# 56 tokens' expert value rows gathered and summed on VectorE instead of 48, in three groups with an accumulator each

## The chip, the cores and the metric

The kernel runs on one core of one Trainium2 chip. The metric is the device time of one execution in microseconds (us). The core has five engines that run their own instruction streams and wait for one another through semaphores: TensorE (PE), VectorE (DVE), ScalarE (ACT), GpSimd (POOL) and SyncE (SP, which here only issues transfers). Transfers run on 16 DMA engines, whichever engine issues them.

## The reference

One decoder layer on 256 tokens of width 1024: a mixer (a gated recurrence and causal attention side by side), cross-attention to 256 memory tokens, and a PEER block, with a final RMSNorm. The change is in PEER, where each token picks, in 8 heads, the 16 best of 128 x 128 = 16384 single-neuron experts:

```
q = (t @ w_q).reshape(T, 8, 2, 128)
s = einsum('thpd,hpnd->thpn', q, sub_keys)        # scores against two sets of 128 keys
ids, gates = top-16 of the 16 x 16 sums of the best 16 of each set; softmax   # 128 ids a token
act = gelu(einsum('td,ted->te', t, u[ids]))        # 128 activations a token
y   = einsum('te,ted->td', gates * act, v[ids])    # sum of 128 value rows a token
```

## The kernel before, in words

Up to about 245 us the kernel computes mixer, cross-attention, queries and key scores; in this part weights are split into a high and a low float32r part, so that three products give float32 accuracy. Then come two passes over all 16384 experts, in 128 steps ("keys") of 128 experts each.

**u pass.** For each key j a 512 KB slab of expert rows is loaded (`raw`, four slots, L373), split into a high part on ACT (L762) and a low part on DVE (L1150), and multiplied with all tokens on PE (L1635 to L1668). ACT applies gelu and leaves activations of the first DT tokens in `act_w` and of the last NS tokens in `act_s`. Meanwhile DVE chooses each token's experts, and POOL scatters the gates of WT = 192 of the tokens into the HBM map `wmap`, with a chain of 192 indirect transfers (L478). The gates of OT = 16 more tokens do not go through the map: PE builds them from one-hots, GRP = 4 tokens at a time (`route`, L1660; `onehots_i`, `onehots_j`, `place`, `late_gelu`).

**v pass.** For each key j a slab of value rows is loaded (L406, issued four keys ahead, when the slab's slot is split), split by ACT (L762) and DVE (`split_low`, L1143), and PE adds, in 8 chunks of 128 output columns, value rows times weighted activations: a matmul of 2 x DT columns (L1702, high and low activations at once) and one of DT columns (L1703, the low part of the rows), 208 each time before the change. The weighted activations are made two keys at a time: SP loads a block of the map (`wblk`, L397), DVE multiplies it in (`weigh`, L1272), ACT and DVE split the product (`a_high` L814, `a_low` L1264). DVE's order for step j is: at odd j `weigh`, then `split_low` of key j + 4, at even j `a_low`, then at some steps one `sparse_fma`.

**The NS sparse tokens** (48 before) do not go through PE. Their 128 experts each are laid out over 128 partitions, so that one column c holds 128 (token, expert) choices: NSD = NS columns. For each column POOL gathers 128 value rows from HBM, 512 KB in all, into one of three slots (`vg`, L501), and one activation for each choice out of the dump of `act_s` (`aw_s`, L492); DVE adds weight times row to an accumulator (L1284, a fused multiply-add; the first column of a group L1286). POOL issues two activation gathers ahead of each value gather until all are out, and starts on `vg` of column c when the sum of column c - 3 is done. When DVE takes a column is fixed by the step:

```
def fma_step(c):
    return FMA0 + c * (KEYS - 8 - FMA0) // NSD      # FMA0 = 12, KEYS = 128
```

There are two groups, of 32 and 16 tokens: a token's choices then lie on 4 or on 8 partitions. After the last column two transfers and two additions fold both accumulators into one (L416, L1342), and in key KEYS - 3 a float32 matmul of 48 columns per chunk sums over the partitions with the 0/1 matrix `sel` (L1724). The last two keys are done chunk by chunk with three matmuls of DT columns each (L1713), followed by residual, norm and output.

**What orders the start of the v pass.** POOL waits until all scatters have landed, then loads the first two map blocks (L486); DVE's first two `weigh` wait for them, and PE's first v matmul for what ACT and DVE make of them.

Of the kernel before, what the change touches and what calls it, by code (L numbers as in the profile page):

```python
# [15 lines left out]
U32 = mybir.dt.uint32  # L16
# [6 lines left out]
P = 128  # L23
# [34 lines left out]
DVE_EVAC = set(range(U_OUT, U_CV3)) | set(range(U_CO, U_PQ))  # L58

GRP = 4  # L60
NS, NSA = 48, 32
NSB = NS - NSA
DT = T - NS
HT = 64
OT = P - HT - NS
NGRP = OT // GRP
WT = P + HT
NDA, NDB = NSA * PH * TOPK // P, NSB * PH * TOPK // P
NSD = NDA + NDB
ACTB = 8  # L70
DUMP = 8
XR2_KEY = KEYS - 16
# [17 lines left out]
def build(nc, x, mem, par, wa, wx, w, keys_t, u_t, v, wmap, adump, sgate, sidx, xres, out):  # L90
    ctx = ExitStack()
    with ctx:
# [8 lines left out]
        K = 1024  # L101

        act_s = at("act_s", 0, [KEYS, NS])
        act_w = at("act_w", 24 * K, [KEYS, DT])
        vg = at("vg", 0, [NVG, D])
        acc_s = at("acc_s", 12 * K, [2, D])
        shifted = at("shifted", 20 * K, [D])
        fin = at("fin", 24 * K, [DC, T])
        ysq = at("ysq", 32 * K, [DC, T])
        orow = at("orow", 40 * K, [TT, D])  # L110
# [23 lines left out]
        oh_j = at("oh_j", m + 4 * K, [2, GRP, P])  # L134
        m += 8 * K
        kt3 = at("kt3", m, [3, OT])
        gate_s = at("gate_s", m + 192, [NSD])
        idx_v = at("idx_v", m + 384, [NSD], U32)
        idx_a = at("idx_a", m + 576, [NSD], U32)
        late = at("late", m + 768, [2, OT])  # L140
        aw_s = at("aw_s", m + 896, [NSD])
        w_s = at("w_s", m + 1088, [NSD])
        stage_g = at("stage_g", m + 1280, [PH * TOPK])
        stage_i = at("stage_i", m + 1792, [PH * TOPK], U32)
        sel = at("sel", m + 4352, [NS])
# [170 lines left out]
        def vbank(c):  # L316

            return acc[:, c] if c < 4 else bank[c - 4]

        SPARSE = ((P - NS, NSA, 0, NDA), (P - NSB, NSB, NDA, NDB))  # L320

        def placed(j):

# [6 lines left out]
        def _(sp):  # L330
# [40 lines left out]
            for j in range(4, KEYS):  # L371
                sp.wait_ge(s_ul, j - 3)
                sp.dma_start(raw[:, j // 2 % 2, j % 2], u_t[j // 2][:, j % 2]).then_inc(s_raw[j % 4], 16)  # L373
                if j == 88:
                    sp.wait_ge(s_stg, 1)
                    for far, near in ((sgate, stage_g), (sidx, stage_i)):
                        for t0, nt, c0, nc_ in SPARSE:
                            sp.dma_start(far[P * c0:P * (c0 + nc_), :].rearrange("(r t c) o -> t r (c o)", t=nt, c=nc_),
                                         near[t0:t0 + nt, :].rearrange("t (r c) -> t r c", c=nc_)).then_inc(s_sst, 16)
                if j == 96:  # L380
                    sp.wait_ge(s_sst, 64)
                    for far, near in ((sgate, gate_s), (sidx, idx_v)):
                        for t0, nt, c0, nc_ in SPARSE:
                            sp.dma_start(near[:, c0:c0 + nc_],
                                         far[P * c0:P * (c0 + nc_), :].rearrange("(p c) o -> p (c o)", p=P)).then_inc(s_sbk, 16)
                if j % DUMP == 0 and j >= 3 * DUMP:
                    dump(j - 3 * DUMP, j - 2 * DUMP)
                if j == KEYS - 4:
                    dump(KEYS - 3 * DUMP, KEYS - 2 * DUMP)
# [37 lines left out]
        def _(pool):  # L427
# [53 lines left out]

            for k, (_, _, _, nr) in enumerate(SETS):
                pool.wait_ge(s_sca[k], 16 * nr * PH)
            pool.wait_ge(s_sst, 64)
            for p in range(2):
                nc.gpsimd.dma_start(wblk[:, p], wm[:, WBK * p:WBK * p + WBK]).then_inc(s_wbp[p], 16)  # L486
            pool.wait_ge(s_ad, 16 * KEYS // DUMP)
# [393 lines left out]
        def _(dve):  # L881
# [86 lines left out]
            dve.wait_ge(s_const, 11)  # L968
            link(V.tensor_copy(posu[:, 0, 0:1], tcol[:, 0:1]))
            V.tensor_scalar(posu[:, 1, 0:1], posu[:, 0, 0:1], NSA - 1, None, ALU.bitwise_and)  # L970
            link(V.tensor_scalar(posu[:, 1, 1:2], posu[:, 0, 0:1], NSB - 1, None, ALU.bitwise_and))
            V.tensor_copy(tcol[:, 2:3], posu[:, 1, 0:1])
            link(V.tensor_copy(tcol[:, 4:5], posu[:, 1, 1:2]))
            V.tensor_scalar(tcol[:, 5:6], tcol[:, 4:5], float(NSA), None, ALU.add)
            link(V.memset(sel[:], 0.0))
            V.tensor_scalar(sel[0:64, 0:NSA], iota[0:64, 0:NSA], tcol[0:64, 2:3], None, ALU.is_equal)
            V.tensor_scalar(sel[64:P, NSA:NS], iota[64:P, 0:NSB], tcol[64:P, 4:5], None, ALU.is_equal)

            dve.wait_ge(s_spc, 1)
            e, z, z2, q, sp8 = c4(1), c4(2), c4(3), c4(4), c4(5)  # L980
# [293 lines left out]
            def sparse_fma(c):  # L1274
                if c % ACTB == 0:
                    cs = slice(c, min(c + ACTB, NSD))
                    dve.wait_ge(s_ag[c // ACTB], 16 * (cs.stop - cs.start))
                    V.tensor_tensor(w_s[:, cs], gate_s[:, cs], aw_s[:, cs], ALU.mult).then_inc(s_ws, 1)
                    dve.wait_ge(s_ws, c // ACTB + 1)
                dve.wait_ge(s_vg[c % NVG], 16 * (c // NVG + 1))  # L1280
                w, to = w_s[:, c:c + 1], acc_s[:, c // NDA]
                if c % NDA:
                    dve.wait_ge(s_fma, c)
                    V.scalar_tensor_tensor(to, vg[:, c % NVG], w, to, ALU.mult, ALU.add).then_inc(s_fma, 1)  # L1284
                else:
                    V.tensor_scalar(to, vg[:, c % NVG], w, None, ALU.mult).then_inc(s_fma, 1)  # L1286
# [8 lines left out]
            for j in range(KEYS):  # L1295
                if j >= WIDE0:
                    wide_sum(j)
                if HALVES <= j < KEYS - 4:
                    split_low_halves(j % 4, s_ul, (s_uh, j + 5))
                elif j < KEYS - 4:  # L1300
                    split_low(j % 4, s_ul, (s_uh, j + 5))
                elif j < KEYS - 1:
                    split_low(j % 4, s_vl, (s_vh, j + 5 - KEYS), second=True)
                if batches < len(BATCHES) and j == batch_key(batches) + 4:
                    gates(batches)
                    batches += 1
                if parts < 4 * TT * PH and j == part_key(parts):
                    route_part(parts // 4, parts % 4)
                    parts += 1
                if j in range(ROUTE0, ROUTE0 + 2 * NGRP, 2):  # L1310
                    place((j - ROUTE0) // 2)
                if placed(j):
                    late_gelu(j)
                if j == ROUTE0 - 2:
                    dve.wait_ge(s_kte, 1)
                if j == ROUTE0 + 2 * NGRP:
                    dve.wait_ge(s_sbk, 64)
                    for (_, _, c0, nc_), col in zip(SPARSE, (2, 5)):
                        cs = slice(c0, c0 + nc_)
                        last = V.tensor_scalar(idx_a[:, cs], idx_v[:, cs], float(NS), tcol[:, col:col + 1], ALU.mult, ALU.add)  # L1320
                    last.then_inc(s_ix, 1)
                if j + 2 in range(ROUTE0, ROUTE0 + 2 * NGRP, 2):
                    onehots_i((j + 2 - ROUTE0) // 2)
                if j == KEYS - 4:
                    for p in range(2):
                        weigh(p)
                if j == KEYS - 3:
                    for p in range(2):
                        a_low(p)
# [54 lines left out]
        def _(pe):  # L1384
# [336 lines left out]
                return last  # L1721

            def sparse_sum(c):
                pe.matmul(vbank(c)[:, DT:T], acc_s[:, 0, P * c:P * c + P], sel[:], start=False, stop=False, skip_group_check=True)  # L1724

            for j in range(8):
                pe.wait_ge(s_vl, j + 1)
# [76 lines left out]
```

## Time and profile before

| | us |
|---|---|
| median of 3 runs (lowest, highest) | 969.2 (968.04, 970.23) |
| the profiled execution's own time | 968.83 |
| its span, first to last instruction | 967.0 |
| PE busy | 954.4 |
| DVE busy | 806.9 |
| ACT busy | 542.6 |
| POOL busy | 486.4 |

The time of an execution is the span plus 1.83 us around it. Busy times are unions over the whole span. A matmul's duration overlaps the next one's, so what a matmul costs is read from start to start. The granted clock of PE is a share of full speed.

### The profile page before, as it was taken

How to read it: one execution, taken by the hardware profiler on the slowest of the kernel's cores; microseconds unless marked ns; L12 is line 12 of the kernel's file. 1: busy time of each engine (PE TensorE's matmuls, PEld its weight loads, DVE VectorE, ACT ScalarE, POOL GpSimd, SP SyncE). 2: the span in 40 equal slices, each digit the busy share in tenths (PEclk: the TensorE clock that was granted, in tenths of full speed). 3: DMA queues.
4: the chain of work that ended last, by engine and by line, in shares of the span. 5: the costliest groups of instructions: out<-in, count | busy, mean ns of one | idle time of the engine just before them, and what ended most of it. 6: DMA issues, size and time to landing. Idle time of an engine off the chain costs nothing.

```text
span 967.0 us, 18013 instructions
## 1 busy us (share of the span) xinstructions
PE 954.4 (99%) x6807; PEld 915.2 (95%) x6807; DVE 806.9 (83%) x1571; ACT 542.6 (56%) x953; POOL 486.4 (50%) x315
## 2 busy tenths in 40 slices
PE   8999999999999999999999999999999999999997
PEld 8897799999999999999998888889999999999997
DVE  5988866446999999999988787777899899999897
ACT  7775546555555546464465565545555455555456
POOL 1001001001488888888788888827478872242210
PEclk9999999999999999999999999999999999999999
DMA  9699865434547787878878878878999999999992
GB/s 317 218 316 323 269 226 200 147 123 139 175 82 203 180 208 179 213 169 205 202 189 208 194 174 194 201 202 307 329 362 345 338 347 374 361 372 354 366 339 95
DMA packets 134265, 235.61 MB, mean 244 GB/s; under 512 B 38624, under 2 KB 87520, under 8 KB 133824
## 3 DMA queue, kind: packets, MB, share of 16 engines
q1 hardware_dynamic: 97552, 208.66, 64.4%
q0 software_dynamic: 36224, 25.70, 14.1%
q8 instruction: 27, 0.44, 0.2%
q10 hardware_dynamic: 432, 0.57, 0.2%
q14 instruction: 30, 0.25, 0.1%
HBM read 216.38 MB, written 17.97 MB: 242 GB/s over the span
## 4 chain that ended last, share of the span: by engine, by line
PE 51%; POOL 33%; issue 8%; DVE 5%; ACT 2%; DMA 1%; ACTq 0%; POOLq 0%; DVEq 0%
POOL wmap L478 33%; PE acc L1702 11%; PE bank L1702 11%; PE acc L1438 11%; PE bank L1703 5%; PE acc L1703 5%; PE acc L1420 3%; DVE wsp L893 1%; PE acc L1421 1%; PE acc L1424 1%; ACT wsp L511 1%; PE bank L1544 1%; PE bank L1391 1%; DMA wmap<-gate,widx 1%; PE bank L1566 1%
## 5 line engine op out<-in xcount | busy, mean ns | idle before, releaser
L478 POOL DMA_INDIRECT wmap<-gate,widx x192 | 322.3, 1679 | 90.8 <-issue 60.0
L762 ACT ACTIVATE hl<-raw 128x1024 fp32r<-128x1024 f32 x192 | 202.3, 1058 | 80.3 <-PE bank L1668 41.7
L1143 DVE TENSOR_TENSOR hl<-raw,hl 128x1024 fp32r<-128x1024 f32 x99 | 120.9, 1221 | 24.2 <-ACT hl L762 24.1
L1635 PE MATMUL bank<-xt,hl 128*128 128x256 f32 x480 | 136.0, 283 | 0.0
L1636 PE MATMUL bank<-xt,hl 128*128 128x256 f32 x480 | 135.9, 283 | 0.0
L1637 PE MATMUL bank<-xt,hl 128*128 128x256 f32 x480 | 135.9, 283 | 0.0
L501 POOL DMA_INDIRECT vg<-v,idx_v x48 | 74.3, 1549 | 119.0 <-DVE acc_s L1284 99.7
L1150 DVE TENSOR_TENSOR hl<-raw,hl 128x512 fp32r<-128x512 f32 x186 | 119.3, 687 | 17.0 <-ACT hl L762 15.8
L1702 PE MATMUL bank<-whl,hl 128*128 128x416 f32 x380 | 121.1, 369 | 0.7 <-DVE acc L1292 0.7
L1702 PE MATMUL acc<-whl,hl 128*128 128x416 f32 x380 | 121.7, 371 | 0.0
L1667 PE MATMUL bank<-xt,hl 128*128 128x512 f32 x288 | 102.4, 399 | 0.0
L893 DVE TENSOR_TENSOR wsp<-wraw,wsp 128x2048 fp32r<-128x2048 f32 x34 | 77.8, 2289 | 24.6 <-ACT wsp L511 24.3
L1703 PE MATMUL bank<-whl,hl 128*128 128x208 f32 x380 | 98.1, 258 | 0.0
L1703 PE MATMUL acc<-whl,hl 128*128 128x208 f32 x380 | 97.9, 258 | 0.0
L511 ACT ACTIVATE wsp<-wraw 128x2048 fp32r<-128x2048 f32 x35 | 67.0, 1914 | 54.0 <-PE acc L1421 24.6
L1636 PEld LDWEIGHTS bank<-xt,hl 128*128 128x128 f32 x480 | 92.1, 192 | 0.0
L1637 PEld LDWEIGHTS bank<-xt,hl 128*128 128x128 f32 x480 | 92.1, 192 | 0.0
L1635 PEld LDWEIGHTS bank<-xt,hl 128*128 128x128 f32 x480 | 92.0, 192 | 0.0
L1438 PE MATMUL acc<-xt,wsp 128*128 128x256 f32 x672 | 84.0, 285 | 0.1
L772 ACT ACTIVATE act_w<-bank 128x208 f32<-128x208 f32 x80 | 27.6, 344 | 99.1 <-PE bank L1637 98.7
L492 POOL DMA_INDIRECT aw_s<-adump,idx_a x48 | 69.6, 1450 | 26.6 <-issue 14.3
L1438 PEld LDWEIGHTS acc<-xt,wsp 128*128 128x128 f32 x672 | 81.6, 192 | 0.7 <-issue 0.4
(306 smaller groups left out, 2379.6 us busy)
## 6 DMA issues: line engine op xcount, KB each, us to landing
raw<-u_t SPq DMA_DIRECT2D x128, 512.0 KB, 4.5
raw<-v SPq DMA_DIRECT2D x128, 512.0 KB, 5.9
wmap<-zeros SPq DMA_DIRECT2D x6, 2048.0 KB, 11.7
wblk<-wmap SPq DMA_DIRECT2D x62, 192.0 KB, 6.1
wraw<-w_in SPq DMA_DIRECT2D x9, 1024.0 KB, 9.4
wraw<-w_pq SPq DMA_DIRECT2D x8, 1024.0 KB, 5.3
wraw<-w_ck SPq DMA_DIRECT2D x4, 1024.0 KB, 8.4
wraw<-w_cv SPq DMA_DIRECT2D x4, 1024.0 KB, 7.0
```

The costliest lines, as they stand in the source:

```text
L478: nc.gpsimd.indirect_dma_start(out=wmap, out_offset=bass.IndirectOffsetOnAxis(ap=set_ranks(widx, k)[:, h, r:r + 1], axis=0), in_=set_ranks ...
L762: nc.scalar.activation(eslot(k, 0, second), raw[:, k // 2, k % 2], ACT.Copy).then_inc(ready, 1)
L893: V.tensor_tensor(wsp[:, u % 2, 1], wraw[:, u % WRAW], wsp[:, u % 2, 0].bitcast(F32), ALU.subtract).then_inc(s_wl, 1)
L1143: V.tensor_tensor(eslot(k, 1, second), raw[:, k // 2, k % 2], eslot(k, 0, second).bitcast(F32), ALU.subtract).then_inc(ready, 1)
L1150: last = V.tensor_tensor(eslot(k, 1, False)[:, q], raw[:, k // 2, k % 2, q], eslot(k, 0, False)[:, q].bitcast(F32), ALU.subtract)
L1438: last = pe.matmul(dst, a, b, start=(c == c0 and n == 0), stop=(c == c1 - 1 and n == 2))
L1635: pe.matmul(dst, uh[:, c], xt[:, c, 0], start=(c == 0), stop=False)
L1636: pe.matmul(dst, uh[:, c], xt[:, c, 1], start=False, stop=False)
L1637: last = pe.matmul(dst, ul[:, c], xt[:, c, 0], start=False, stop=(c == DC - 1))
L1667: pe.matmul(dst, uh[:, c], flat(xt[:, c]), start=(c == 0), stop=False, skip_group_check=True)
L1702: pe.matmul(both, vh[:, q], whole, start=first, stop=False, skip_group_check=True)
L1703: last = pe.matmul(both[:, 0], vl[:, q], whole[:, 0], start=False, stop=False, skip_group_check=True)
```

## The change

Eight more tokens move from PE to the sparse path: NS goes from 48 to 56, so DT from 208 to 200, and a third group of 8 tokens (each on 16 partitions) gets its own accumulator, staging transfers and columns of `sel`. The tokens placed by one-hots, OT = 128 - 64 - NS, go from 16 to 8, so NGRP from 4 to 2. The map's width WT stays. `sparse_sum` becomes two matmuls, of 48 and of 8 columns, since the third accumulator is not folded into the first. Some tiles move in SBUF. The index step that stood at ROUTE0 + 2 * NGRP = 103 keeps its place as ROUTE0 + 8. `fma_step` is unchanged but divides by the new NSD = 56.

```diff
--- before.py
+++ after.py
@@ -58,15 +58,15 @@
 DVE_EVAC = set(range(U_OUT, U_CV3)) | set(range(U_CO, U_PQ))
 
 GRP = 4
-NS, NSA = 48, 32
-NSB = NS - NSA
+NS, NSA, NSB, NSC = 56, 32, 16, 8
 DT = T - NS
 HT = 64
 OT = P - HT - NS
 NGRP = OT // GRP
 WT = P + HT
-NDA, NDB = NSA * PH * TOPK // P, NSB * PH * TOPK // P
-NSD = NDA + NDB
+NDA, NDB, NDC = (n * PH * TOPK // P for n in (NSA, NSB, NSC))
+NSD = NDA + NDB + NDC
+FIRSTS = (0, NDA, NDA + NDB)
 ACTB = 8
 DUMP = 8
 XR2_KEY = KEYS - 16
@@ -101,10 +101,10 @@
         K = 1024
 
         act_s = at("act_s", 0, [KEYS, NS])
-        act_w = at("act_w", 24 * K, [KEYS, DT])
+        act_w = at("act_w", 28 * K, [KEYS, DT])
         vg = at("vg", 0, [NVG, D])
-        acc_s = at("acc_s", 12 * K, [2, D])
-        shifted = at("shifted", 20 * K, [D])
+        acc_s = at("acc_s", 12 * K, [3, D])
+        shifted = at("shifted", 24 * K, [D])
         fin = at("fin", 24 * K, [DC, T])
         ysq = at("ysq", 32 * K, [DC, T])
         orow = at("orow", 40 * K, [TT, D])
@@ -134,12 +134,12 @@
         oh_j = at("oh_j", m + 4 * K, [2, GRP, P])
         m += 8 * K
         kt3 = at("kt3", m, [3, OT])
-        gate_s = at("gate_s", m + 192, [NSD])
-        idx_v = at("idx_v", m + 384, [NSD], U32)
-        idx_a = at("idx_a", m + 576, [NSD], U32)
+        gate_s = at("gate_s", m + 96, [NSD])
+        idx_v = at("idx_v", m + 320, [NSD], U32)
+        idx_a = at("idx_a", m + 544, [NSD], U32)
         late = at("late", m + 768, [2, OT])
-        aw_s = at("aw_s", m + 896, [NSD])
-        w_s = at("w_s", m + 1088, [NSD])
+        aw_s = at("aw_s", m + 832, [NSD])
+        w_s = at("w_s", m + 1056, [NSD])
         stage_g = at("stage_g", m + 1280, [PH * TOPK])
         stage_i = at("stage_i", m + 1792, [PH * TOPK], U32)
         sel = at("sel", m + 4352, [NS])
@@ -317,7 +317,7 @@
 
             return acc[:, c] if c < 4 else bank[c - 4]
 
-        SPARSE = ((P - NS, NSA, 0, NDA), (P - NSB, NSB, NDA, NDB))
+        SPARSE = ((P - NS, NSA, 0, NDA), (P - NSB - NSC, NSB, NDA, NDB), (P - NSC, NSC, NDA + NDB, NDC))
 
         def placed(j):
 
@@ -378,7 +378,7 @@
                             sp.dma_start(far[P * c0:P * (c0 + nc_), :].rearrange("(r t c) o -> t r (c o)", t=nt, c=nc_),
                                          near[t0:t0 + nt, :].rearrange("t (r c) -> t r c", c=nc_)).then_inc(s_sst, 16)
                 if j == 96:
-                    sp.wait_ge(s_sst, 64)
+                    sp.wait_ge(s_sst, 32 * len(SPARSE))
                     for far, near in ((sgate, gate_s), (sidx, idx_v)):
                         for t0, nt, c0, nc_ in SPARSE:
                             sp.dma_start(near[:, c0:c0 + nc_],
@@ -481,7 +481,7 @@
 
             for k, (_, _, _, nr) in enumerate(SETS):
                 pool.wait_ge(s_sca[k], 16 * nr * PH)
-            pool.wait_ge(s_sst, 64)
+            pool.wait_ge(s_sst, 32 * len(SPARSE))
             for p in range(2):
                 nc.gpsimd.dma_start(wblk[:, p], wm[:, WBK * p:WBK * p + WBK]).then_inc(s_wbp[p], 16)
             pool.wait_ge(s_ad, 16 * KEYS // DUMP)
@@ -968,13 +968,17 @@
             dve.wait_ge(s_const, 11)
             link(V.tensor_copy(posu[:, 0, 0:1], tcol[:, 0:1]))
             V.tensor_scalar(posu[:, 1, 0:1], posu[:, 0, 0:1], NSA - 1, None, ALU.bitwise_and)
-            link(V.tensor_scalar(posu[:, 1, 1:2], posu[:, 0, 0:1], NSB - 1, None, ALU.bitwise_and))
+            V.tensor_scalar(posu[:, 1, 1:2], posu[:, 0, 0:1], NSB - 1, None, ALU.bitwise_and)
+            link(V.tensor_scalar(posu[:, 1, 2:3], posu[:, 0, 0:1], NSC - 1, None, ALU.bitwise_and))
             V.tensor_copy(tcol[:, 2:3], posu[:, 1, 0:1])
-            link(V.tensor_copy(tcol[:, 4:5], posu[:, 1, 1:2]))
+            V.tensor_copy(tcol[:, 4:5], posu[:, 1, 1:2])
+            link(V.tensor_copy(tcol[:, 6:7], posu[:, 1, 2:3]))
             V.tensor_scalar(tcol[:, 5:6], tcol[:, 4:5], float(NSA), None, ALU.add)
+            V.tensor_scalar(tcol[:, 7:8], tcol[:, 6:7], float(NSA + NSB), None, ALU.add)
             link(V.memset(sel[:], 0.0))
             V.tensor_scalar(sel[0:64, 0:NSA], iota[0:64, 0:NSA], tcol[0:64, 2:3], None, ALU.is_equal)
-            V.tensor_scalar(sel[64:P, NSA:NS], iota[64:P, 0:NSB], tcol[64:P, 4:5], None, ALU.is_equal)
+            V.tensor_scalar(sel[64:P, NSA:NSA + NSB], iota[64:P, 0:NSB], tcol[64:P, 4:5], None, ALU.is_equal)
+            V.tensor_scalar(sel[:, NSA + NSB:NS], iota[:, 0:NSC], tcol[:, 6:7], None, ALU.is_equal)
 
             dve.wait_ge(s_spc, 1)
             e, z, z2, q, sp8 = c4(1), c4(2), c4(3), c4(4), c4(5)
@@ -1278,8 +1282,8 @@
                     V.tensor_tensor(w_s[:, cs], gate_s[:, cs], aw_s[:, cs], ALU.mult).then_inc(s_ws, 1)
                     dve.wait_ge(s_ws, c // ACTB + 1)
                 dve.wait_ge(s_vg[c % NVG], 16 * (c // NVG + 1))
-                w, to = w_s[:, c:c + 1], acc_s[:, c // NDA]
-                if c % NDA:
+                w, to = w_s[:, c:c + 1], acc_s[:, sum(c >= f for f in FIRSTS) - 1]
+                if c not in FIRSTS:
                     dve.wait_ge(s_fma, c)
                     V.scalar_tensor_tensor(to, vg[:, c % NVG], w, to, ALU.mult, ALU.add).then_inc(s_fma, 1)
                 else:
@@ -1313,9 +1317,9 @@
                     late_gelu(j)
                 if j == ROUTE0 - 2:
                     dve.wait_ge(s_kte, 1)
-                if j == ROUTE0 + 2 * NGRP:
-                    dve.wait_ge(s_sbk, 64)
-                    for (_, _, c0, nc_), col in zip(SPARSE, (2, 5)):
+                if j == ROUTE0 + 8:
+                    dve.wait_ge(s_sbk, 32 * len(SPARSE))
+                    for (_, _, c0, nc_), col in zip(SPARSE, (2, 5, 7)):
                         cs = slice(c0, c0 + nc_)
                         last = V.tensor_scalar(idx_a[:, cs], idx_v[:, cs], float(NS), tcol[:, col:col + 1], ALU.mult, ALU.add)
                     last.then_inc(s_ix, 1)
@@ -1721,7 +1725,9 @@
                 return last
 
             def sparse_sum(c):
-                pe.matmul(vbank(c)[:, DT:T], acc_s[:, 0, P * c:P * c + P], sel[:], start=False, stop=False, skip_group_check=True)
+                q = slice(P * c, P * c + P)
+                pe.matmul(vbank(c)[:, DT:T - NSC], acc_s[:, 0, q], sel[:, 0:NS - NSC], start=False, stop=False, skip_group_check=True)
+                pe.matmul(vbank(c)[:, T - NSC:T], acc_s[:, 2, q], sel[:, NS - NSC:NS], start=False, stop=False, skip_group_check=True)
 
             for j in range(8):
                 pe.wait_ge(s_vl, j + 1)
```

## Rows read from the trace of the kernel before

**Rows 1.** The page, part 1: busy time, share of the span and instructions of each engine.
```profile
PE 954.4 (99%) x6807; PEld 915.2 (95%) x6807; DVE 806.9 (83%) x1571; ACT 542.6 (56%) x953; POOL 486.4 (50%) x315
```

**Rows 2.** Stretches: PE, PEld, DVE, ACT, POOL busy (count), PE clock, DMA share, GB/s.
```profile
690.00:934.00 244.00, 244.00 (x1625) 242.49 (x1624) 221.26 (x253) 131.19 (x152) 123.46 (x80) 1.00 0.97 356
...
860.00:880.00 20.00, 20.00 (x135) 19.89 (x134) 17.34 (x21) 10.79 (x13) 3.03 (x3) 1.00 1.00 384
```

**Rows 3.** Waits from 690 to 934 us: us in total, times, longest.
```profile
ACT hl L762 <- DMA raw<-v: 23.7, 25, 3.0
...
DVE hl L1143 <- ACT hl L762: 16.8, 30, 1.5
...
ACT hl L762 <- PE bank L1703: 4.4, 5, 1.3
```

**Rows 4.** Timeline of PE: start and duration in us, line, tiles, shapes, count.
```profile
499.81 0.28 PE L1635 MATMUL bank<-xt,hl 128*128 128x256 f32 x1
...
504.84 0.28 PE L1635 MATMUL bank<-xt,hl 128*128 128x256 f32 x1
...
606.14 0.40 PE L1667 MATMUL bank<-xt,hl 128*128 128x512 f32 x1
...
611.09 0.40 PE L1667 MATMUL bank<-xt,hl3u 128*128 128x512 f32 x1
...
802.64 0.37 PE L1702 MATMUL acc<-whl,hl 128*128 128x416 f32 x1
...
922.95 0.45 PE L1702 MATMUL acc<-whl,hl 128*128 128x416 f32 x1
...
947.06 0.37 PE L1702 MATMUL acc<-whl,hl 128*128 128x416 f32 x1
...
949.62 0.44 PE L1702 MATMUL acc<-whl,hl 128*128 128x416 f32 x1
...
950.15 0.43 PE L1702 MATMUL acc<-whl,hl 128*128 128x416 f32 x1
...
953.67 0.50 PE L1713 MATMUL acc<-whl,hl 128*128 128x208 f32 x3
...
958.70 0.50 PE L1713 MATMUL bank<-whl,hl3v 128*128 128x208 f32 x3
```

**Rows 5.** Timeline of DVE in the v pass.
```profile
685.14 0.55 DVE L1272 TENSOR_TENSOR act_w<-act_w,wblk 128x384 f32<-128x384 f32 x1
...
690.10 0.55 DVE L1272 TENSOR_TENSOR act_w<-act_w,wblk 128x384 f32<-128x384 f32 x1
...
743.29 0.55 DVE L1272 TENSOR_TENSOR act_w<-act_w,wblk 128x384 f32<-128x384 f32 x1
...
747.05 0.55 DVE L1272 TENSOR_TENSOR act_w<-act_w,wblk 128x384 f32<-128x384 f32 x1
...
751.49 0.55 DVE L1272 TENSOR_TENSOR act_w<-act_w,wblk 128x384 f32<-128x384 f32 x1
...
921.59 1.23 DVE L1143 TENSOR_TENSOR hl<-raw,hl 128x1024 fp32r<-128x1024 f32 x1 [1.48 <-ACT hl L762]
...
941.18 0.55 DVE L1272 TENSOR_TENSOR act_w<-act_w,wblk 128x384 f32<-128x384 f32 x1
```

**Rows 6.** Timeline of POOL (GpSimd) in the v pass.
```profile
715.66 4.13 POOL L501 DMA_INDIRECT vg<-v,idx_v  x1 [0.30 <-issue]
...
724.66 0.95 POOL L501 DMA_INDIRECT vg<-v,idx_v  x1 [0.31 <-issue]
...
792.60 1.80 POOL L501 DMA_INDIRECT vg<-v,idx_v  x1 [0.30 <-issue]
```

**Rows 7.** Timeline of PE and DVE: last routing matmuls, change from u to v pass.
```profile
573.17 1.06 PE L1660 MATMUL acc<-oh_j,oh_i 128*128 128x128 f32 x8
...
643.86 1.14 DVE L1272 TENSOR_TENSOR act_w<-act_w,wblk 128x384 f32<-128x384 f32 x2 [2.21 <-DMA wblk<-wmap]
...
647.47 0.38 PE L1702 MATMUL acc<-whl,hl 128*128 128x416 f32 x1
```

## Prediction

> **What bounds the kernel now.** I read the page first: TensorE (PE) is busy for 99% of the span and VectorE (DVE) for 83% [rows 1], which says little until it is split by stage. The view by stretches does that for the last third, the v pass, where the change works: in 244 us PE is busy throughout at full clock, DVE for 221 us, the DMA engines for 97% at 356 GB/s [rows 2]. Three resources are near full at once, so I asked for the waits of the same stretch: PE waits for nothing, but ScalarE (ACT) waits 25 times for a value row from HBM, and DVE 30 times for ACT [rows 3]. So the chain that feeds PE (load, high part on ACT, low part on DVE) is hardly faster than PE. The timelines show how little is in hand: the low part of one key was done at 921.59 + 1.23 = 922.82 [rows 5], and PE began on it at 922.95 [rows 4]. PE sets the end only with 0.13 us to spare.
>
> **PE's saving.** From 802.64 to 947.06 lie 60 keys of 8 pairs [rows 4]: 144.42 / 480 = 300.9 ns for a pair of 416 and 208 columns, 2.407 us a key. Both shrink, to 400 and 200. Two other shapes price a column. 42 matmuls of 256 columns take 5.03 us, 119.8 ns each; 15 triples of 208 columns take 5.03 us, 111.8 ns each [rows 4]. So a short matmul gives back 8.0 ns for 48 columns, 0.17 ns a column: it is nearly at a floor, and 8 columns give 1.3 ns. The pair of 512 and 256 takes (611.09 - 606.14) / 14 = 353.6 ns [rows 4]; take off 300.9 and the 8.0, and 96 columns of the long one cost 44.7 ns, 0.466 a column: 16 give 7.5 ns. Together 8.8 ns, and 126 keys x 8 pairs give 8.9 us. Bounds: 7.5 us if the short one is at its floor, 11.7 if a pair shrinks in proportion (24 / 624 of 300.9). I take 8.9, as measured shapes lie on both sides; a key then takes 2.337 us.
>
> **PE's new work.** In the third key from the end each chunk also adds the sparse sums: chunks follow one another in 950.15 - 949.62 = 0.53 us [rows 4] instead of 0.30, so the matmul of 48 columns costs 0.23 us, far more than its columns at 0.466. The third group needs a second such matmul, of 8 columns, with weights of its own. Between nothing and 0.23 us I take 0.23, since so little of the first one's cost is columns: 8 x 0.23 = +1.8 us. The last two keys' triples give 16 x 3 x 1.3 ns, under 0.1 us.
>
> **DVE's new work.** Eight more fused multiply-adds (FMA) of 128x1024, and what counts is where fma_step puts them. DVE works in periods of two keys, from one weigh (L1272) to the next: weigh, split, split, a_low. Three kinds can be read [rows 5]:
> - no FMA: 743.29 to 747.05, 3.76 us
> - FMA between the two splits (odd step): 747.05 to 751.49, 4.44 us, no gap
> - FMA behind the second split (even step): 685.14 to 690.10, 4.96 us, since DVE also stands idle between the splits while ACT finishes.
>
> With 48 FMAs, fma_step gives 23 even, 24 odd and 6 empty periods in the 53 periods of steps 13 to 118. Their floors add up to 23 x 4.96 + 24 x 4.44 + 6 x 3.76 = 243.2 us; they took 941.18 - 685.14 = 256.0 us [rows 5]. The 12.8 us above the floors are late loads (rows, wblk, gathers), and at a few places PE holding the splits back: ACT waited for it 5 times, 4.4 us in all [rows 3]. Less than half of that, 1.7 us, I take as DVE's, which a DVE that is behind would not lose; 11.1 us remain. PE's 106 keys took 255.1 us. The two were even.
>
> With 56 FMAs the same formula gives 25 even, 26 odd, 2 with both, and none empty; and they come in runs of 13, not of 4. Floors: a_low loses 16 of 416 columns, 0.02 us of its half microsecond, so 25 x 4.93 + 26 x 4.42 + 2 x (4.42 + 1.20) = 249.4 us, where 1.20 is what an even period with an FMA has over an empty one, 4.96 - 3.76. PE would need 106 x 2.337 = 247.7: DVE's floor alone is above that. What the late loads add is not in the trace. Below: nothing, if the longer periods cover them. Above: every added byte delays: 8 gathers of 128 rows of 4 KB are 4.19 MB, 11.8 us at 356 GB/s, so 256.0 + 11.8 = 267.8. I keep the 11.1 us of before, since the DMA share was near its end already and the loads have the same slots: 249.4 + 11.1 = 260.5 us, +4.5.
>
> How much of that reaches PE: at the end of these periods DVE was ahead, since the next split ended at 941.18 + 0.55 + 1.23 = 942.96, and PE began that key at 947.06 - 2.41 = 944.65 [rows 4, 5]: 1.7 us, of which all but 0.15 can be used up. So +4.5 - 1.55 = +2.95 at that key; PE's faster pace is lost in waits before it. Behind it three keys save 0.2.
>
> **Edits at nothing.** In the u pass two of four routing groups go, at most 1.06 us of PE each [rows 7]. But the v pass cannot begin before the scattered gates are back: DVE waited 2.21 us for wblk at 643.86, and PE's first v matmul at 647.47 follows what DVE does after that [rows 7]; PE only waits longer there. Were that cover gone, 2.1 us would be gained. Four more small loads and stores on SP at keys 88 and 96, with a longer wait there, hold up the u rows queued behind them; SP runs four keys ahead, so nothing, at most one landing like the 2.21 us. The five new one-column instructions on DVE in the first stage are each under the 0.55 us of a weigh [rows 5]; under PE's work nothing, uncovered 2.8 us at most. The act dump grows by a sixth, before gathers that then wait for the first FMA anyway.
>
> **Sum.** +2.95 - 0.2 + 1.8 - 0.1 = +4.45 us on the profiled execution's own 968.83 (967.0 span, 1.83 around it; the median of the runs, 969.2, is 0.4 above): 973.3, so **973**. This case reaches from 971 to 977.
>
> **Rivals.**
> *PE keeps the pace (faster).* If the longer periods hide the late loads, DVE needs its 249.4 us, 1.55 us of which the lead pays, and PE's saving arrives: -8.9 + 1.8 = -7.1, **961.7**; with half of it 965. For it: with a run of 13 odd periods DVE gets ahead at 4.42 against PE's 4.67. Against: the periods of before lay 11.1 us above their floors, and the traffic grows. It decides at a mean period of 4.70 us; before it was 4.83.
>
> *Traffic binds (much slower).* DMA engines at 97% [rows 2] may have no more to give: 267.8 instead of 256.0 is +11.8 - 1.55 - 0.3 + 1.8 = +11.75, **980.6**. For it: the share. Against: 384 GB/s in one stretch of 20 us [rows 2], 8% above the mean. The Trainium skill speaks against the change here: its page DMA: Bandwidth & Descriptors, section Specifications, sets some 358 GB/s of HBM for a core. By that rule this rival would be certain; the trace's 384 disagrees.
>
> *GpSimd's gathers come late (slower).* Each FMA needs one value row gather and, up to the 28th, two act gathers. Where DVE runs without a gap a gather took 4.13 us [rows 6], and three took (792.60 - 724.66) / 13 = 5.23 us [rows 6] in the stretch with all three. The first run of 13 odd periods asks for three in 4.42 to 4.7: up to 13 x 0.6 = 8 us more of DVE waiting, which with 4.45 gives up to 981, **979** with most of it. For it: only 4 odd periods stood in a row before. Against: three gathered rows in hand, and any wait of DVE opens the gap. The Trainium skill has the mechanism: SBUF — State Buffer, section SBUF: two separate sides, says that GpSimd and some DVE instructions exclude each other at a shared port, so that DMAs whose descriptors GpSimd writes starve; the 4.13 us agree.
>
> *Nothing measurable.* If half of the 11.1 us is hidden, DVE takes 255.0, and -1.0 - 1.55 - 0.3 + 1.8 = -1.05, **968**.
>
> **Chances.** This forecast 0.52, traffic 0.10, gathers 0.08, nothing measurable 0.14, PE keeps the pace 0.16. A measurement of this kernel tells about 0.2%, 1.9 us, from no change: faster 0.17, same 0.15, slower 0.68. The range, 965 to 981, leaves out most of the full PE gain (0.11) and what lies beyond the two slow rivals (0.08).
>
> **What would show it.** Right: v pairs near 292 ns where PE does not wait; waits of PE for DVE's splits, 10 us or so in all, most in the runs of even steps; mean period near 4.9 us; first v matmul still near 647.4; chunk spacing with sparse sums near 0.75 us. Wrong: no waits of PE and a mean period of 4.7 (first rival); DMA share of 1.00 with 356 GB/s (traffic); DVE waiting for vg in steps 13 to 39 (gathers); pairs at 289 ns (columns of the short matmul do count).

## The result, and the profile after

The changed kernel took **985.7 us** (median of 6 executions, 978.9 to 994.9) against 968.6 us for the kernel before: a ratio of **1.0163 [1.0139, 1.0188]**. The sign was forecast and the size was not: 973.0 had been given, with 981 as the upper end. One of the six executions, the one of 994.9, fell into a slower state of the chip; the ratio leaves it out, and without it the median is 981.9. The profiled execution took 981.93 us, 13.1 more than that of before.

Part 1 of the page of the changed kernel, which answers to [rows 1]:

```profile
PE 956.7 (98%) x6807; PEld 914.3 (93%) x6807; DVE 811.9 (83%) x1573; ACT 537.6 (55%) x943; POOL 504.6 (51%) x331
```

PE's busy time hardly moved; what is new is that PE stands idle. The view by stretches, for the same part of the v pass as [rows 2] and for three short stretches in it (columns as there):

```profile
690.00:948.00 258.00, 248.96 (x1635) 244.63 (x1635) 228.92 (x261) 130.02 (x151) 142.11 (x95) 0.98 0.97 354
...
756.00:760.00 4.00, 3.60 (x17) 3.22 (x16) 3.59 (x4) 2.43 (x3) 3.08 (x4) 0.57 0.68 243
760.00:764.00 4.00, 4.00 (x18) 3.98 (x18) 3.75 (x6) 1.32 (x2) 3.39 (x3) 0.57 0.97 356
764.00:768.00 4.00, 4.00 (x29) 4.00 (x28) 3.79 (x5) 1.51 (x3) 3.32 (x3) 1.00 0.94 315
```

In 258 us PE was idle for 9.0 us, where it had been idle for none. In two of the short stretches its granted clock was 0.57, and it got through 17 and 18 matmuls instead of 29. The waits of the same stretch (us in total, times, longest), beside [rows 3]:

```profile
ACT hl L762 <- DMA raw<-v: 26.6, 29, 4.8
...
DVE acc_s L1288 <- DMA vg<-v,idx_v: 9.8, 8, 4.5
PE acc L1706 <- DVE hl L1147: 8.5, 6, 3.1
...
DVE act_w L1276 <- DMA wblk<-wmap: 7.0, 5, 2.5
```

Two rows are the news: PE waits for DVE's splits, which it did not do before in this part, and DVE waits 9.8 us for gathered value rows (`vg`), 2.4 us before. The timeline of DVE gives the 53 periods of steps 13 to 118, first and last `weigh`, the longest wait for `vg`, and the `weigh` at 756.98 with which the first 14 periods end:

```profile
682.78 0.55 DVE L1276 TENSOR_TENSOR act_w<-act_w,wblk 128x384 f32<-128x384 f32 x1
...
752.44 1.28 DVE L1288 SCALAR_TENSOR_TENSOR acc_s<-vg,w_s,acc_s 128x1024 f32<-128x1024 f32 x1 [4.54 <-DMA vg<-v,idx_v]
...
756.98 0.55 DVE L1276 TENSOR_TENSOR act_w<-act_w,wblk 128x384 f32<-128x384 f32 x1
...
953.37 0.55 DVE L1276 TENSOR_TENSOR act_w<-act_w,wblk 128x384 f32<-128x384 f32 x1
```

953.37 - 682.78 = 270.6 us, against 256.0 [rows 5]. That is the whole result: the first `weigh` is 2.4 us earlier than before, the periods take 14.6 longer, and from the last `weigh` to the end of the span it is 26.7 us instead of 25.8 (967.0 - 941.18). -2.4 + 14.6 + 0.9 = +13.1. The first 14 periods, with 9.3 of the 9.8 us of waits for `vg`, took 756.98 - 682.78 = 74.2 us, 7.9 more than before (751.49 - 685.14 [rows 5]); the other 39 took 6.7 more.

Why `vg` is late can be read in the timeline of GpSimd (POOL), where the first run of 13 odd periods ends. It answers to [rows 6]:

```profile
719.60 1.31 POOL L501 DMA_INDIRECT vg<-v,idx_v  x1 [0.30 <-issue]
...
722.81 4.12 POOL L492 DMA_INDIRECT aw_s<-adump,idx_a  x1 [0.30 <-issue]
727.24 1.18 POOL L501 DMA_INDIRECT vg<-v,idx_v  x1 [0.30 <-issue]
...
739.30 4.12 POOL L492 DMA_INDIRECT aw_s<-adump,idx_a  x1 [0.30 <-issue]
743.73 1.77 POOL L501 DMA_INDIRECT vg<-v,idx_v  x1 [0.30 <-issue]
...
752.78 1.76 POOL L501 DMA_INDIRECT vg<-v,idx_v  x1 [0.31 <-issue]
```

From 719.60 to 752.78 there are six steps from one value gather to the next, 5.53 us each, with two act gathers in each and never a wait for DVE. DVE asks for a row every 4.42 us. GpSimd cannot keep up, the three slots run dry, and DVE stops. Then PE does, and its clock falls. The timeline of PE:

```profile
646.67 0.42 PE L1706 MATMUL acc<-whl,hl 128*128 128x400 f32 x1 [0.35 <-issue]
...
738.78 0.37 PE L1706 MATMUL bank<-whl,hl 128*128 128x400 f32 x1
...
748.20 0.37 PE L1706 MATMUL bank<-whl,hl 128*128 128x400 f32 x1
...
755.00 0.44 PE L1706 MATMUL acc<-whl,hl 128*128 128x400 f32 x1 [3.11 <-DVE hl L1147]
...
930.20 0.45 PE L1706 MATMUL acc<-whl,hl 128*128 128x400 f32 x1 [2.90 <-DVE hl L1147]
...
961.59 0.33 PE L1729 MATMUL acc<-sel,acc_s 128*128 128x48 f32 x2
...
966.04 0.34 PE L1729 MATMUL bank<-sel,acc_s 128*128 128x48 f32 x2
```

Between 738.78 and 748.20 lie four keys without a wait: 9.42 / 32 = 294.4 ns a pair. The wait of 3.11 us at 755.00 stands directly ahead of the stretch at 0.57. The second long wait, 2.90 us at 930.20, is not one for gathers: ahead of it ACT waited 4.8 us for a value row and DVE 2.5 us for a map block, the longest waits of their rows above.

### The profile page after: what moved, and what is told of

Its sections match the earlier page's. It is cut to its first block, busy times and chain, and to the rows that moved or that the text cites. A ratio compares the mean times of both kernels' runs of the same rounds, so it can differ in the third digit from the quotient of the medians.

```text
span 980.1 us, 18029 instructions
## 1 busy us (share of the span) xinstructions
PE 956.7 (98%) x6807; PEld 914.3 (93%) x6807; DVE 811.9 (83%) x1573; ACT 537.6 (55%) x943; POOL 504.6 (51%) x331
## 4 chain that ended last, share of the span: by engine, by line
POOL 40%; PE 20%; DVE 14%; issue 12%; DMA 9%; ACT 4%; SPq 0%; ACTq 0%; POOLq 0%; DVEq 0%
POOL wmap L478 32%; PE acc L1442 10%; POOL aw_s L492 6%; DMA wblk<-wmap 4%; DMA raw<-v 3%; POOL vg L501 3%; DVE acc_s L1288 2%; DVE hl L1147 2%; DVE wsp L893 2%; ACT hl L762 2%; DVE whl L1268 1%; DMA wmap<-gate,widx 1%; PE acc L1424 1%; DVE act_w L1276 1%; PE acc L1706 1%
## 5 line engine op out<-in xcount | busy, mean ns | idle before, releaser
L501 POOL DMA_INDIRECT vg<-v,idx_v x56 | 83.9, 1499 | 106.9 <-DVE acc_s L1288 84.8
L1706 PE MATMUL acc<-whl,hl 128*128 128x400 f32 x380 | 122.0, 372 | 8.9 <-DVE hl L1147 8.5
L1706 PE MATMUL bank<-whl,hl 128*128 128x400 f32 x380 | 121.7, 372 | 0.7 <-DVE acc L1296 0.7
L1707 PE MATMUL bank<-whl,hl 128*128 128x200 f32 x380 | 97.7, 257 | 0.0
L1707 PE MATMUL acc<-whl,hl 128*128 128x200 f32 x380 | 97.6, 257 | 0.0
L492 POOL DMA_INDIRECT aw_s<-adump,idx_a x56 | 81.0, 1447 | 31.2 <-issue 16.8
L1706 PEld LDWEIGHTS acc<-whl,hl 128*128 128x128 f32 x380 | 72.5, 191 | 12.2 <-DVE hl L1147 8.3
```

Of the source, the lines that this page charges most:

```text
L492: nc.gpsimd.indirect_dma_start(out=aw_s[:, c:c + 1], out_offset=None, in_=adump, in_offset=bass.IndirectOffsetOnAxis(ap=idx_a[:, c:c + 1], ...
L501: nc.gpsimd.indirect_dma_start(out=vg[:, c % NVG], out_offset=None, in_=v, in_offset=bass.IndirectOffsetOnAxis(ap=idx_v[:, c:c + 1], axis= ...
L1706: pe.matmul(both, vh[:, q], whole, start=first, stop=False, skip_group_check=True)
L1707: last = pe.matmul(both[:, 0], vl[:, q], whole[:, 0], start=False, stop=False, skip_group_check=True)
```

## The experiments

Two theories stood against each other from the start. *Gathers late*: GpSimd issues too many gathers where DVE is dense. *Traffic*: eight more rows' bytes are what costs. DVE's period floors (4.42 and 4.93 us) were the third. Medians over all executions, and the ratio to the kernel before on the same chip:

| run | what | us (lowest to highest) | ratio |
|---|---|---|---|
| e1_spread | act gathers spread | 974.7 (973.7–977.7) | 1.0067 [1.0047, 1.0087] |
| e2_no_act_rows | 48 act gathers left out | 974.6 (971.2–980.7) | 1.0063 [1.0040, 1.0086] |
| e5_pe_only | PE's shapes, 48 FMAs | 966.2 (963.9–974.3) | 0.9979 [0.9953, 1.0006] |
| e6_supply_only | before with 8 more gathers, FMAs | 984.5 (971.1–992.4) | 1.0184 [1.0133, 1.0235] |
| e3_odd_spread | odd steps to 119, spread | 975.7 (974.0–987.2) | 1.0108 [1.0038, 1.0177] |
| e4_even_spread | even steps, spread | 981.5 (978.8–985.3) | 1.0122 [1.0075, 1.0170] |
| e9_no_bytes | spread, 8 rows not gathered | 970.1 (966.8–975.9) | 1.0014 [0.9982, 1.0046] |
| e10_no_fma | spread, 8 FMAs cut | 970.0 (965.7–973.8) | 1.0011 [0.9991, 1.0031] |
| e11_odd_early | odd steps 9 to 113, spread | 972.9 (965.5–979.8) | 1.0031 [1.0007, 1.0055] |
| e12_odd_early_xr2 | and residual load late | 973.6 (966.8–977.5) | 1.0032 [1.0011, 1.0054] |
| e13_spread_xr2 | e1 and residual load late | 972.8 (970.2–979.8) | 1.0044 [1.0016, 1.0071] |
| e14_before_odd_xr2 | before with odd steps, spread, residual load late | 968.6 (967.1–970.2) | 0.9989 [0.9971, 1.0007] |
| e15_odd_no_act | e11, 48 act gathers left out | 967.6 (963.9–970.5) | 0.9992 [0.9976, 1.0007] |
| e16_odd_slots | odd, spread, five slots | 968.9 (963.9–972.1) | 1.0004 [0.9988, 1.0020] |
| e17_slots_spread | five slots, spread, steps of the change | 974.2 (973.3–975.3) | 1.0061 [1.0040, 1.0082] |
| e18_slots | the change with five slots | 986.9 (982.3–994.8) | 1.0216 [1.0180, 1.0251] |
| e19_dense_start | e16, first FMAs closer | 971.5 (967.3–975.5) | 1.0025 [1.0004, 1.0046] |
| e20_odd_slots_no_bytes | e16, 8 rows not gathered | 965.4 (963.1–968.9) | 0.9965 [0.9947, 0.9984] |

**e1_spread.**

```
-                if c >= NVG:
-                    act_rows(ACTB + 2 * (c - NVG), ACTB + 2 * (c - NVG + 1))
+                if c == NVG:
+                    act_rows(ACTB, 2 * ACTB)
+                elif c > NVG:
+                    act_rows(2 * ACTB + c - NVG - 1, 2 * ACTB + c - NVG)
```

> All 56 FMAs, all gathers; only GpSimd's order changes: 8 act gathers move into the 9.9 us in which it stood idle before the first FMA, and the rest goes one per FMA instead of two. Theory 'gathers late' (three gathers per FMA are too many for GpSimd in the first odd run): the waits of DVE for vg in steps 13 to 40, 9.8 us, vanish, and most of it reaches the end: 977 to 980. Theory 'traffic' (the HBM bytes of eight more rows gathered are the price, whoever issues them): the bytes are the same, so 984 to 987, with the waits moved to other loads.

Measured 974.7, less than either forecast: by the ratios (1.0163 - 1.0067) x 968.6 = 9.3 us came back, by the medians 11.0, for an order of the same instructions. Its timeline of DVE, first and last `weigh` of the 53 periods and the one behind the first 14:

```profile
684.21 0.55 DVE L1278 TENSOR_TENSOR act_w<-act_w,wblk 128x384 f32<-128x384 f32 x1
...
752.27 0.55 DVE L1278 TENSOR_TENSOR act_w<-act_w,wblk 128x384 f32<-128x384 f32 x1
...
945.28 0.55 DVE L1278 TENSOR_TENSOR act_w<-act_w,wblk 128x384 f32<-128x384 f32 x1
```

261.1 us instead of 270.6, and its waits hold no row for `vg`. Gathers late is right for this part. Of the 9.5 us, 6.1 lie in the first 14 periods (68.1 instead of 74.2 us); the other 3.4 lie behind them, where even the changed kernel hardly waits for `vg`, and how they hang on the gathers was not shown.

**e2_no_act_rows.** (`act_rows` only for the first eight columns; `w_s` made from `aw_s[:, 0:ACTB]` each time.)

> Leaves out 48 of the 56 act gathers: every group of eight value rows is weighted with the first group's act values. GpSimd then has one gather per FMA. Theory 'gathers late': no wait for vg, 975 to 979, a little below the spread order. Theory 'traffic': the act gathers move 512 bytes each, so the time stays at 983 to 986.

974.6, the same as with the gathers spread: 48 act gathers cost nothing that can be told once they are out of the way.

**e5_pe_only.** (`NF = NDA + NDB` in place of `NSD` for gathers, FMAs and steps.)

> The changed layout (400 and 200 columns, two matmuls in the sparse sum) with the 48 FMAs, the gathers and the places of before: the third group's eight rows are not gathered or summed, and its matmul reads the second accumulator. If PE's shapes alone count: 6.6 us saved by 6.5 ns a pair, 1.8 us lost in the sparse sum, 968.6 - 4.8 = 963.8. If DVE was already as much the bound as PE before the change: 966 to 969, with waits of PE for DVE's splits of 3 to 6 us.

966.2, the number of the second forecast: PE's shapes save 2.8 us by the medians and 2.0 by the ratio, not 4.8. Its interval reaches 1.0006, so the saving alone is just not told from nothing. The forecast's reason is not in the trace: from 690 to 937 PE was idle for 0.3 us only, and a pair took some 297 ns (246.71 us busy for 1661 matmuls) instead of 294.4. Why is open. The rise from here to e1, 8.5 us, is the price of the third group's gathers and FMAs when they are well ordered.

**e6_supply_only.** (The kernel before with `NX = NSD + 8` in `fma_step`, the gathers and the FMAs; `vcol(c) = c - 8` for the last eight.)

> The kernel before, with eight more value row gathers and FMAs on DVE (the last eight columns a second time) at the 56 places of the changed kernel; no act gathers for them, PE's shapes as before. Theory 'gathers late': the two act gathers per FMA end at the same count as before, PE is slower than in the changed kernel, 973 to 978. Theory 'traffic': 4.19 MB at 356 GB/s is 11.8 us on 968.6: 979 to 981. Theory 'DVE's period floors': PE needs 106 x 2.407 = 255.1 us, DVE 249.4 + 11.1 = 260.5, less 1.55 of lead: 971 to 973.

984.5, above every forecast, but from four executions that lie 21 us apart. The one with a trace took 971.1, and there DVE waited only 1.1 us for `vg` and PE 1.1 us for DVE's splits. Of the longer ones there is no trace, so this run settles nothing.

**e3_odd_spread and e4_even_spread.**

```
-            return FMA0 + c * (KEYS - 8 - FMA0) // NSD
+            return 9 + 2 * c          # e4: 8 + 2 * c
```

> GpSimd's act gathers spread as in the first experiment (974.7), and every FMA put into an odd step (9, 11, ... 119), between the two splits of a period; nothing else differs. Theory 'DVE's period floors' (what remains over the PE part alone, 966.2, is DVE losing time in even periods and in the two double ones): all periods have a floor of 4.42 us, 53 x 4.42 = 234.3 instead of 249.4, so PE keeps the pace and the time is that of the PE part alone, 963 to 967. Theory 'traffic' (the eight extra rows' bytes are what remains): 973 to 976, as before.

> The same with every FMA in an even step (8, 10, ... 118), behind the second split. Theory 'DVE's period floors': 53 x 4.93 = 261.3 us of floor against 249.4, 12 more, of which the late loads may cover half: 980 to 987. Theory 'traffic': 973 to 976.

Even steps took 981.5, 7 us more: the floors count. Odd steps took 975.7, no less than the mixture. From 690 to 930 the odd kernel is what the theory wants (first row below: PE busy for 240.0 of 240 us), and then it loses all of it. Its view by stretches, a wait of SP's queue from 915 to 950, and ACT's timeline:

```profile
690.00:930.00 240.00, 240.00 (x1632) 240.00 (x1632) 226.19 (x260) 131.28 (x151) 174.00 (x90) 1.00 1.01 379
```
```profile
948.00:952.00 4.00, 4.00 (x19) 3.99 (x18) 1.81 (x5) 1.76 (x6) 0.00 (x0) 0.50 0.01 4
```
```profile
SPq L416 <- DVE acc_s L1290: 5.3, 1, 5.3
```
```profile
944.65 1.06 ACT L764 ACTIVATE hl<-raw 128x1024 fp32r<-128x1024 f32 x1 [6.08 <-DMA raw<-v]
```

The last FMA, at step 119, is one that SP waits for before it stores the sums, and two value slabs are queued behind that store. They came 6.1 us late, PE waited 2.5 us, and its granted clock was 0.50 afterwards. That was a fault of the experiment's steps.

**e9_no_bytes and e10_no_fma.**

```
+OWN = [c for c in range(NSD) if c % 7 != 5]     # e9: the others are not gathered
+                    some = slice(0, 8 if c % 7 == 5 else D)     # e10: width of the FMA
```

> Spread act gathers; DVE does all 56 FMAs at the same places, but the rows of 8 columns (every seventh) are not gathered: their FMAs read the slot of the column ahead of them a second time. That takes away 4.19 MB and 8 value gathers of GpSimd, and no work of DVE. Theory 'traffic': 4.19 MB at 371 GB/s is 11.3 us of the DMA engines, so the time falls to that of the PE part alone, 965 to 968. Theory 'DVE's period floors': no change, 973 to 976.

> Spread act gathers; all 56 rows are gathered, but the FMAs of 8 columns (every seventh) work on 8 of their 1024 elements: all bytes, and some 8 x 1.1 us less work on DVE. Theory 'DVE's period floors': 965 to 968. Theory 'traffic': no change, 973 to 976. If both count in part, this run and the one without the bytes each fall by a part.

970.1 and 970.0, between the numbers of both theories: each takes away some 4.6 us of the 8.5, so neither is the whole of it. The rows to be fetched and DVE's time each count for about half. e9 takes away the bytes of 8 rows and GpSimd's issue of them together, so it does not tell which of the two counts.

**e11_odd_early, e12_odd_early_xr2.** (`sorted([*range(9, 114, 2), 40, 66, 92])[c]`; e12 also `XR2_KEY = KEYS - 2`.)

> Spread act gathers and odd steps again, but the FMAs end earlier: 53 at the odd steps 9 to 113 and three more at the even steps 40, 66 and 92. In the run with odd steps up to 119, SP waited 5.3 us for the last FMA ahead of its store of the sums, with the value rows of keys 126 and 127 queued behind it; ACT then waited 6.1 us for them, PE 2.5 us for the fold, and TensorE's granted clock fell to 0.50 for the last 17 us. Theory 'DVE's period floors, and then SP's queue': that is gone and PE keeps the pace all through, 962 to 966. Theory 'traffic': the missing rows were late because the DMA engines are full, so the lateness moves elsewhere: 970 to 975.

> As the run before, with the load of the 1 MB residual moved from key 112 to key 126, behind the last value rows. If that load costs wblk and value rows their time (waits of 1.1 and 3.0 us at 930 in the run with odd steps): 0 to 3 us less than the run before, nothing if the lead covers it. If it comes too late for the residual adds: 1 to 3 us more.

972.9 and 973.6, and executions 11 to 14 us apart. 972.9 is what traffic forecast, 970 to 975; the late residual load changes nothing that can be told. But the timelines of GpSimd and of DVE in e11 show another place than the DMA engines:

```profile
682.80 1.78 POOL L492 DMA_INDIRECT aw_s<-adump,idx_a  x1 [0.30 <-issue]
684.88 4.12 POOL L503 DMA_INDIRECT vg<-v,idx_v  x1 [0.31 <-issue]
```
```profile
696.15 1.28 DVE L1290 SCALAR_TENSOR_TENSOR acc_s<-vg,w_s,acc_s 128x1024 f32<-128x1024 f32 x1 [7.96 <-DMA vg<-v,idx_v]
```

The fourth value gather stood behind eight act gathers, and then took 4.12 us while DVE had no gap. DVE waited 8.0 us for that row. So the number was right for traffic and its reason was not, as e15 shows.

**e13_spread_xr2, e14_before_odd_xr2.**

> The first experiment (spread act gathers, FMAs where the change puts them, 974.7) with the residual load moved to key 126. Theory 'the residual load makes the long period near 928': 2 to 3 us less, 971 to 973. Else 974 to 976.

> The kernel before with its 48 FMAs at the odd steps 9 to 103, spread act gathers and the residual load at key 126: the same care without the change. PE was busy through 99.9% of the v pass in the kernel before, so almost nothing is to be gained: 966.5 to 969. If the kernel before lost time to DVE that its busy share hides: 962 to 966.

972.8 against e1's 974.7, with intervals that overlap: not shown. The kernel before gains nothing from the same steps, order and late load, 968.6, as expected where PE is the bound.

**e15_odd_no_act.** (e11's steps with e2's weights.)

> The odd-step kernel (FMAs at odd steps 9 to 113, three at even ones), with 48 of the 56 act gathers left out: every group of eight rows is weighted with the first group's act values. It tells why the odd steps did not pay (972.9). Theory 'gathers starve where DVE has no gap': with one gather per 4.42 us period, of at most 4.12 us, GpSimd keeps up, DVE's waits for vg (13.9 us in the odd-step kernel) go, and the time is 963 to 967. Theory 'traffic': the act gathers carry few bytes, 971 to 975.

967.6, 5 us less than e11 and just above what gathers late says: one gather a period can be kept up. Its groups of GpSimd's instructions show how near that is, 2196 ns a gather where DVE is dense, against 1496 in the same stretch of the changed kernel:

```profile
L499 POOL DMA_INDIRECT vg<-v,idx_v x50 | 109.8, 2196 | 113.5 <-DVE acc_s L1286 108.8 <-DVE acc_s L1288 4.7
```

**e16_odd_slots, e17_slots_spread, e18_slots.**

```
+        vg2 = at("vg2", 144 * K, [2, D])              # slots 4 and 5, NVG = 5
+            return sorted([*range(13, 118, 2), 40, 66, 92])[c]     # e16 alone
-                if j == KEYS - 3:
+                if j == KEYS - 12:                    # e16, e17: store of the sums
```

> All the work. Odd steps 13 to 117 with three even ones, spread act gathers, five slots for gathered rows instead of three (two in the space of the residual, whose load moves to key 126), and the store of the first two groups' sums at key 116, as soon as their 48 FMAs are done. Theory 'gathers starve': GpSimd may run five FMAs ahead, so that a starved stretch is bridged: 963 to 968. Theory 'traffic': no bytes less, 970 to 975.

> The same with the FMAs at the steps where the change puts them (runs of odd, then of even steps). Theory 'gathers starve': 969 to 972, the rest being the floors of the even periods; theory 'traffic': 970 to 975. If this one is faster than the odd steps, gaps on DVE are worth more than short periods.

> The changed kernel (985.7) with five slots for gathered rows instead of three and the residual load at key 126, the act gathers two per FMA as the change has them. Theory 'gathers starve': five rows in hand bridge part of the first odd run, 974 to 980; the spread order with three slots took 972.8. Theory 'a third gather per period is simply too much for GpSimd': more slots move the wait a few periods on, 981 to 986.

e16, with all the work, takes 968.9: what the kernel before takes, 15 us less than the change by the ratios, 0.9 above the range of gathers late, and under that of traffic. e17, at 974.2 above the range of gathers late, has gained nothing on e1, so it is odd steps and slots together; both also store the sums earlier and load the residual later, which was not tried by itself with odd steps and five slots. e18 has gained nothing either: with three gathers per FMA more slots are no help. There DVE's 53 periods took 263.8 us (948.9 - 685.1) instead of 270.6, yet they began 2.3 us later, and from the last `weigh` to the end it was 31.6 us instead of 26.7, with PE's clock at half for part of it. Stretches of e16 and, at the end, of e18:

```profile
690.00:930.00 240.00, 239.37 (x1626) 239.09 (x1626) 229.38 (x262) 133.27 (x153) 159.60 (x90) 1.00 1.01 376
```
```profile
956.00:960.00 4.00, 3.70 (x25) 3.70 (x26) 1.47 (x2) 0.88 (x2) 0.00 (x0) 0.84 0.71 283
960.00:964.00 4.00, 4.00 (x19) 3.99 (x19) 2.35 (x5) 3.97 (x9) 0.00 (x0) 0.50 0.00 0
```

e16's profiled execution took 963.9 us with PE all but never idle; others of it took up to 972.1.

**e19_dense_start.** (`sorted([9, 10, 11, 12, *range(13, 115, 2), 64])[c]`.)

> All the work: the five-slot kernel with odd steps (968.9), but the first FMAs earlier and closer, at steps 9 to 13, where DVE waits for PE anyway, then the odd steps 15 to 113 and step 64. It gives GpSimd and DVE about one period in hand. If what is left (963.9 to 972.1 from one execution to the next) is gathers and FMAs that come late, 964 to 967. If it is the DMA engines, which moved 375 GB/s at a share of 1.01 there, 967 to 970 as before.

971.5, neither number. In its profiled execution DVE used up the five rows at once and then waited 7.6 us for the sixth, as in e11: a miss that shows the same cause, and a bad way to ask the question.

**e20_odd_slots_no_bytes.** (e16 with e9's edit.)

> The five-slot kernel with odd steps (968.9; its executions 963.9 to 972.1) without the gathers of 8 value rows, whose FMAs read the row of the column ahead of them a second time: 4.19 MB and 8 of GpSimd's gathers less, all of DVE's work kept. Theory 'what is left is transfers' (the DMA engines full, loads and gathers late now and then): the median falls to 964 to 966 and the executions lie within 3 us. Theory 'DVE's work': 967 to 970, as wide as before.

965.4, 3.5 us less than e16, with executions 6 us apart rather than 8, and the only run surely faster than the kernel before, with work left out. What is left in e16 is mostly the rows to be fetched (their bytes or their issue by GpSimd, which this run takes away together). DVE's work is hardly it: all 56 FMAs are still there, and the time is that of e5 with 48.

## Why the prediction was wrong in size

- **PE's saving**: forecast 8.9 us, 8.8 ns a pair. Measured 300.9 - 294.4 = 6.5 ns, 6.6 us for 126 keys, so the term was 2.3 too large. How the 6.5 divides between the long and the short matmul was not shown.
- **The sparse sum's second matmul**: forecast chunks 0.75 us apart; (966.04 - 961.59) / 6 = 0.742. Right.
- **Floors**: 4.93 for the even periods. Right, and e4 shows that they are paid. DVE's floor as the bound was right in kind.
- **The step that failed** is "I keep the 11.1 us of before": 249.4 + 11.1 = 260.5 us for the 53 periods. They took 270.6, 21.2 above their floors. e1 shows what the 11.1 was worth: with the gathers spread the same 53 periods at the same steps took 261.1, 11.7 above the floors, and the kernel 974.7 us, 1.7 from the forecast. So a sum of about the size of before's excess did come again, though no run shows that it has the same causes, and 9.5 us came on top that an order of gathers takes away. The forecast had put those at nothing.
- **The rival was named, and kept out of the sum.** GpSimd's gathers had 979, up to 8 us more than the forecast, and a chance of 0.08. The price was near, 9.5 us; the chance was not. Its sign, DVE waiting for `vg` in steps 13 to 39, is there. Three gathers took 5.53 us instead of the 5.23 read before. The long gathers were not more: over 3.5 us took 6 before and 5 after, from 690 to 930; there was no time left to make them good. "Any wait of DVE opens the gap" was true and came too late: the wait itself is the loss. The Trainium skill, page SBUF — State Buffer, section SBUF: two separate sides, has GpSimd and some DVE instructions exclude each other at a shared port; the 4.12 us beside 0.95 agree, and so do the 2196 ns of e15, but no run here singles out the port.
- **Traffic** was half right. It was not the cause of what e1 gave back, for the bytes there are the same; but e9 gives the eight rows, with their issue, half of the 8.5 that the third group costs with its gathers spread. As a hard limit at 356 GB/s it falls: e16 moved 376 over 240 us. By the Trainium skill, page DMA: Bandwidth & Descriptors, section Specifications, a core has about 358; the measurement decides against it here.
- **v start**: forecast about 647.4, measured 646.67. The forecast had PE waiting there for the scattered gates, so that less work ahead would gain nothing; but [rows 7] show no wait of PE at 647.47, and 0.8 us was gained.
- **Not in the sum at all**: the clock. A wait of PE of 3.1 us was followed by 8 us at 0.57. The mean granted clock was 0.998 in the profiled execution of before, 0.994 in that of after: (0.998 - 0.994) x 980 = 3.9 us at most. Among the others of after the clock goes with the time: 978.9 and 981.5 us at 0.997, 989.4 and 990.0 at 0.994. Reckoned the same way the clock is 0.003 x 985 = 3 us of that difference of some 9.5, and the profiled execution, at 0.994 too, took 981.9. What its share is was not shown; no run held it fixed.

By the ratios the 1.63% divide into -0.21 for PE's part (e5), +0.88 for the third group's rows and FMAs (e1 - e5) and +0.96 for the order of the gathers (after - e1): -2.0, +8.5 and +9.3 us. They add up by the way they are taken, so that is no test of them. Open is why executions of one kernel differ by 8 us and more once its supply is this tight.

## What to carry over

When work is moved from the bound engine to one that is nearly as busy, price what feeds the second engine too, instruction by instruction and over the longest run without a gap, not on average. A surplus that a queue of three slots hides in runs of four periods is a stall in runs of thirteen; spreading the issue cured it, more slots alone did not. Even with everything in place (e16), the change bought nothing: without eight of the rows the kernel was 3.5 us faster (e20), so most of what PE saved seems to have gone into fetching them.

## What was not expected of the hardware

- An indirect gather took GpSimd from 0.95 us to 4.12 us; the mean of the value gathers was 1.50 us in the changed kernel, with DVE busy for 213 of the 240 us from 690 to 930, and 2.20 us in e15, with DVE busy for 228.
- The DMA engines moved 376 to 379 GB/s over 240 us (e16, e3), where 356 had looked like a ceiling.
- After PE's wait of 3.11 us its granted clock showed 0.57 for 8 us, most of that at the lower of its two levels (1.2 instead of 2.4 GHz): from 757.02 to 757.57, 0.55 us a pair instead of 0.294. In e18 PE's one wait from 930 to 965 took 0.7 us, and the clock fell to 0.50 behind it; in e1 the same matmul waited 0.7 us as well, and the clock stayed at 1.00 from 952 to 964. So the length of the wait alone does not decide.
